# Delta rule of an RWKV-7 branch: the first level of the next pair's inverse moved into the pair ahead, and each chunk's level products issued by themselves

## The reference, cut to what matters

```
def rwkv7_scan(r, w, k, v, kk, a):
    """S_t = S_{t-1}(diag(w_t) - kk_t^T (a_t*kk_t)) + v_t^T k_t ; y_t = S_t r_t. All (B,T,H,N)."""
    def step(S, inp):
        r_t, w_t, k_t, v_t, kk_t, a_t = inp
        sa = jnp.einsum('bhvk,bhk->bhv', S, -kk_t)
        S = (S * w_t[:, :, None, :] + sa[..., None] * (kk_t * a_t)[:, :, None, :]
             + v_t[..., None] * k_t[:, :, None, :])
        y = jnp.einsum('bhvk,bhk->bhv', S, r_t)
        return S, y
```

## Time and profile before

| | |
|---|---|
| Median of 3 executions | 1852.13 us (1851.4 to 1854.01) |
| The profiled execution's own time | 1844.2 us |
| Its span, first to last instruction | 1842.4 us |
| Mean granted TensorE clock | 0.985 |
| Busy: PE, PE weight loads, DVE, ACT, POOL | 1730.4, 1366.7, 1136.0, 822.2, 712.8 us |
| Delta rule of layer 0 | 363.93 to 459.93 us of the span |
| Delta rule of layer 1 | 907.53 to about 1005 us of the span |

### The profile page before, as it was taken

One profiled execution on the slowest core, in us unless ns is written; L12 is line 12 of the kernel. 1 busy time (PEld: TensorE's weight loads), 2 busy tenths in 40 slices (PEclk: granted clock), 3 DMA queues, 4 the chain that ended last, 5 costly groups with the idle time before them and its releaser, 6 DMA issues.

```text
span 1842.4 us, 31964 instructions
## 1 busy us (share of the span) xinstructions
PE 1730.4 (94%) x12808; PEld 1366.7 (74%) x12808; DVE 1136.0 (62%) x1515; ACT 822.2 (45%) x1233; POOL 712.8 (39%) x488
## 2 busy tenths in 40 slices
PE   7999999978998999999978997999998999999996
PEld 7778777767776777777777774666777888887875
DVE  6676787775666127977765745568728364636454
ACT  3443655543635344655533625367634333323342
POOL 2565443320343435633310451433444434334342
PEclk9999999999998999999999998999999999999998
DMA  9772222200532422223201422312243212122222
GB/s 359 268 262 79 92 97 87 93 26 4 196 98 78 152 78 80 92 87 104 76 27 57 163 93 88 151 57 69 80 146 129 92 59 86 65 78 80 69 92 103
DMA packets 63188, 193.01 MB, mean 105 GB/s; under 512 B 5936, under 2 KB 6192, under 8 KB 62672
## 3 DMA queue, kind: packets, MB, share of 16 engines
q1 hardware_dynamic: 63056, 191.10, 30.7%
HBM read 173.25 MB, written 17.83 MB: 104 GB/s over the span
## 4 chain that ended last, share of the span: by engine, by line
PE 60%; issue 21%; POOL 8%; DVE 7%; ACT 4%; POOLq 0%; DVEq 0%; ACTq 0%
PE proj L2417 40%; POOL w_lo_sb L705 7%; PE aux L2436 4%; PE aux L2684 2%; DVE area_sb L1415 2%; PE aux L2597 1%; PE aux L2447 1%; DVE slots_sb L1418 1%; PE aux L3135 1%; PE aux L3141 1%; PE proj L2684 1%; PE aux L2458 1%; PE aux L3132 1%; DVE slots_sb L1415 1%; DVE slots_sb L2107 1%
## 5 line engine op out<-in xcount | busy, mean ns | idle before, releaser
L705 POOL TENSOR_TENSOR w_lo_sb<-w_raw_sb,w_hi_sb 128x512 fp32r<-128x512 f32 x462 | 687.8, 1510 | 986.1 <-ACT w_hi_sb L796 986.1
L2417 PE MATMUL proj<-act_hi_sb,w_hi_sb 128*128 128x512 f32 x1480 | 600.7, 406 | 9.1 <-ACT stage_sb L1209 2.6
L2417 PE MATMUL proj<-act_hi_sb,w_lo_sb 128*128 128x512 f32 x1480 | 578.3, 391 | 0.0
L2417 PE MATMUL proj<-act_lo_sb,w_hi_sb 128*128 128x512 f32 x1480 | 576.9, 390 | 0.0
L796 ACT ACTIVATE w_hi_sb<-w_raw_sb 128x1024 fp32r<-128x1024 f32 x231 | 244.2, 1057 | 658.4 <-PE proj L2417 480.7
L2417 PEld LDWEIGHTS proj<-act_hi_sb,w_hi_sb 128*128 128x128 f32 x1480 | 278.3, 188 | 90.7 <-issue 27.8
L2417 PEld LDWEIGHTS proj<-act_lo_sb,w_hi_sb 128*128 128x128 f32 x1480 | 278.6, 188 | 61.8 <-issue 7.7
L2417 PEld LDWEIGHTS proj<-act_hi_sb,w_lo_sb 128*128 128x128 f32 x1480 | 278.1, 188 | 59.8
L2436 PE MATMUL aux<-act_hi_sb,w_hi_sb 128*128 128x512 f32 x336 | 138.1, 411 | 23.7 <-issue 18.2
L1415 DVE TENSOR_TENSOR area_sb<-area_sb 128x256 f32<-128x256 f32 (+1 forms) x180 | 118.1, 699 | 44.6 <-PE aux L2598 26.7
L2436 PE MATMUL aux<-act_lo_sb,w_hi_sb 128*128 128x512 f32 x336 | 133.9, 399 | 0.0
(11 more groups left out here) (316 smaller groups left out, 2293.0 us busy)
## 6 DMA issues: line engine op xcount, KB each, us to landing
w_raw_sb<-wall SPq DMA_DIRECT2D x231, 512.0 KB, 3.4
area_sb<-w_ada SPq DMA_DIRECT2D x32, 512.0 KB, 5.1
slots_sb<-w_ada SPq DMA_DIRECT2D x32, 256.0 KB, 7.4
gate_scr<-stage_sb SPq DMA_DIRECT2D x32, 256.0 KB, 2.2
area_sb<-gate_scr SPq DMA_DIRECT2D x8, 1024.0 KB, 9.0
x_scr<-area_sb SPq DMA_DIRECT2D x3, 2048.0 KB, 7.8
area_sb<-x_scr SPq DMA_DIRECT2D x2, 2048.0 KB, 13.2
area_sb<-lru_gates SPq DMA_DIRECT2D x1, 3584.0 KB, 11.7
```

Source lines behind the costliest of these rows:

```text
L705: nc.gpsimd.tensor_tensor(w_lo[:, b % 2, :, :].rearrange("p k n -> p (k n)")[:, half], w_raw[:, b % 2, half], w_hi[:, b % 2, :, :].rearran ...
L2417: ins = MM(bank, w[:, s, k, :], a[:, t, :], start=(start and i == 0), stop=(stop and i == len(terms) - 1))
```

## The change

Three things change in the delta rule.

First, level 0 of the next pair (its z and x) is computed within the pair ahead of it, and in the opening for the first pair. For that the masked scores `m1` get a third buffer, `mask_scores` of the next pair moves from the end of a pair into its middle, and the banks 2 and 3 (now `NEXT`) hold the next pair's scores and level-0 z.

Second, the level products of the two chunks are no longer one `beside` call on four corners. Each chunk's product is a call of its own on two corners, with its own waits.

Third, the small steps are placed anew: `key_scores` and `mask_keys` early in the pair, `tokens` in two halves that go through bank 4 one after the other, `u_sb` in two buffers, `state_step(c)` after the level-1 x, both outputs after the level-3 z, and on DVE a wait for the copied xt ahead of the first transposes of a pair.

```
--- before.py
+++ after.py
@@ -228,51 +228,55 @@
...
-        INVERSE, TURNED = (0, 1), (2, 3)
+        INVERSE, NEXT = (0, 1), (2, 3)
...
         for n in range(2, RW_CHUNKS, 2):
             c = n - 2
-            both("z", n, 0, banks=INVERSE)
             jobs.add(("rhs", l, c), 6)
-            both("x", n, 0, banks=INVERSE)
+            both("z", n, 1, banks=INVERSE)
+            both("sk", n, banks=NEXT)
             jobs.add(("u", l, c), 5)
-            both("z", n, 1, banks=INVERSE)
+            both("x", n, 1, banks=INVERSE)
             jobs.add(("st", l, c), 7)
-            both("x", n, 1, banks=INVERSE)
+            jobs.add(("tok", l, n, 0), 4)
+            both("z", n, 2, banks=INVERSE)
             jobs.add(("rhs", l, c + 1), 6)
-            both("z", n, 2, banks=INVERSE)
+            if n + 2 < RW_CHUNKS:
+                both("sb", n + 2, banks=NEXT)
+            both("x", n, 2, banks=INVERSE)
+            jobs.add(("tok", l, n, 1), 4)
+            both("z", n, 3, banks=INVERSE)
+            jobs.add(("u", l, c + 1), 5)
             jobs.add(("y", l, c), 4)
-            both("x", n, 2, banks=INVERSE)
             jobs.add(("y", l, c + 1), 6)
-            jobs.add(("u", l, c + 1), 5)
+            both("x", n, 3, banks=INVERSE)
+            if n + 2 < RW_CHUNKS:
+                both("z", n + 2, 0, banks=NEXT)
             jobs.add(("st", l, c + 1), 7)
-            both("z", n, 3, banks=INVERSE)
-            both("sk", n, banks=(4, 5))
-            both("x", n, 3, banks=INVERSE)
-            for m in range(2):
-                jobs.add(("tok", l, n, m), TURNED[m])
             both("z", n, 4, banks=INVERSE)
             if n + 2 < RW_CHUNKS:
-                both("sb", n + 2, banks=(5, 6))
-            both("xt", n, 4, banks=TURNED)
+                both("x", n + 2, 0, banks=INVERSE)
+            both("xt", n, 4, banks=NEXT)
         for name, bank in (("rhs", 6), ("st", 7), ("y", 4), ("u", 5)):
             jobs.add((name, l, RW_CHUNKS - 2), bank)
...
         R_PART, A_PART = slice(0, 64), slice(64, 128)
-        m1 = [[heads(tiles(2 * k + e), P) for e in range(2)] for k in range(2)]
...
         state_end, rhs_sb = (heads(tiles(22)[:, 256 * e:256 * e + 256], 64) for e in range(2))
-        u_sb = heads(tiles(23)[:, 0:256], 64)
...
                 def pair(i):
                     n, c = 2 * i + 2, 2 * i
                     take(rhs_sb, ("rhs", l, c))
-                    grown(n, 0)
-                    take(u_sb, ("u", l, c))
+                    take(u_sb[0], ("u", l, c))
                     grown(n, 1)
+                    tokens_taken(n, 0)
+                    grown(n, 2)
                     take(rhs_sb, ("rhs", l, c + 1))
+                    tokens_taken(n, 1)
+                    take(u_sb[1], ("u", l, c + 1))
+                    grown(n, 3)
                     take_y(c)
-                    grown(n, 2)
-                    take(u_sb, ("u", l, c + 1))
-                    grown(n, 3)
                     take_y(c + 1)
-                    tokens_taken(n)
+                    if n + 2 < RW_CHUNKS:
+                        grown(n + 2, 0)
                     turned_inverse(n)
 
                 def closing(c):
                     take(rhs_sb, ("rhs", l, c))
-                    take(u_sb, ("u", l, c))
+                    take(u_sb[0], ("u", l, c))
                     take_y(c)
                     take(rhs_sb, ("rhs", l, c + 1))
-                    take(u_sb, ("u", l, c + 1))
+                    take(u_sb[1], ("u", l, c + 1))
                     take_y(c + 1)
...
                     grown, across = tiles(8), tiles(9)
+                    if n and k == 0:
+                        for e in range(2):
+                            job_ready(dve, ("xt", l, n - 2 + e, 4))
                     evacuated_job(dve, ("x", l, n, k))
                     nc.vector.transpose(across[:, 0:256], grown[:, 0:256]).then_inc(S("turned"), 1)
                     evacuated_job(dve, ("x", l, n + 1, k))
@@ -1842,31 +1850,35 @@
                     dve.wait_ge(S("ones_set"), 3 * l + 3)
                     turned(0, 2)
                     levels(0, 3)
+                    mask_scores(2)
                     turned(0, 3)
+                    mask_scores(3)
                     levels(0, 4)
-                    mask_scores(2)
-                    mask_scores(3)
+                    levels(2, 0)
 
                 def pair(i):
                     n, c = 2 * i + 2, 2 * i
-                    levels(n, 0)
+                    more = n + 2 < RW_CHUNKS
                     turned(n, 0)
                     levels(n, 1)
+                    mask_keys(n)
+                    mask_keys(n + 1)
                     next_state(c)
                     turned(n, 1)
                     levels(n, 2)
                     end_state(c)
+                    if more:
+                        mask_scores(n + 2)
                     turned(n, 2)
                     levels(n, 3)
+                    if more:
+                        mask_scores(n + 3)
                     next_state(c + 1)
-                    mask_keys(n)
-                    mask_keys(n + 1)
                     turned(n, 3)
+                    if more:
+                        levels(n + 2, 0)
+                    levels(n, 4)
                     end_state(c + 1)
-                    levels(n, 4)
-                    if n + 2 < RW_CHUNKS:
-                        mask_scores(n + 2)
-                        mask_scores(n + 3)
 
...
                 def inverse_level(n, k):
 
-                    names = [("z", l, n + e, k) for e in range(2)]
-                    parts = []
                     for e in range(2):
                         if k:
                             evacuated_job(pe, ("x", l, n + e, k - 1))
@@ -2740,12 +2749,9 @@
                             evacuated_job(pe, ("sb", l, n + e))
                             pe.wait_ge(S("first_turned"), RW_CHUNKS * l + n + e + 1)
                         x = x_next[e] if k else both(x_one[e])[0]
-                        parts.append((job_open(pe, names[e])[:, 0:256], e == 1 and k > 0,
-                                      of(m1[n // 2 % 2][e], A_PART), of(x), True, True))
-                        if k == 0:
-                            signalled(beside(parts[e]), names[e])
-                    if k:
-                        signalled(beside(*parts), *names)
+                        name = ("z", l, n + e, k)
+                        signalled(beside((job_open(pe, name)[:, 0:256], e == 1 and k > 0,
+                                          of(m1[n // 2 % 3][e], A_PART), of(x), True, True)), name)
 
                 def inverse_turned(n, k, e):
...
@@ -2870,56 +2870,62 @@
                     inverse_level(0, 1)
                     values(2)
                     grow(0, 1)
+                    for m in range(2):
+                        tokens(0, m)
                     inverse_level(0, 2)
-                    tokens(0)
                     grow(0, 2)
+                    upper_scores(2)
+                    values(4)
                     inverse_level(0, 3)
-                    values(4)
+                    values(6)
                     grow(0, 3)
-                    values(6)
                     inverse_level(0, 4)
-                    upper_scores(2)
+                    inverse_level(2, 0)
+                    grow(2, 0)
                     turn_inverse(0)
 
                 def pair(i):
                     n, c = 2 * i + 2, 2 * i
-                    inverse_level(n, 0)
+                    more = n + 2 < RW_CHUNKS
                     right_side(c)
-                    grow(n, 0)
+                    inverse_level(n, 1)
+                    key_scores(n)
                     chunk_updates(c)
-                    inverse_level(n, 1)
+                    grow(n, 1)
                     state_step(c)
-                    grow(n, 1)
+                    tokens(n, 0)
+                    inverse_level(n, 2)
 
                     evacuated_job(pe, ("st", l, c))
                     right = half_bank(("rhs", l, c + 1))
                     state_added(beside((right, True, *state_side(c + 1), True, False))[0], c + 1)
-                    inverse_level(n, 2)
+                    if more:
+                        upper_scores(n + 2)
+                    grow(n, 2)
                     after_state(c + 1)
                     signalled(beside((right, False, *keyed_side(c + 1), False, True)), ("rhs", l, c + 1))
+                    tokens(n, 1)
+                    inverse_level(n, 3)
+                    chunk_updates(c + 1)
                     chunk_output(c)
-                    grow(n, 2)
                     out = half_bank(("y", l, c + 1))
                     old_output(c + 1, out)
-                    chunk_updates(c + 1)
-
+                    grow(n, 3)
+                    if more:
+                        inverse_level(n + 2, 0)
+
+                    evacuated_job(pe, ("u", l, c + 1))
```

(10 more changed lines are left out.)

82 lines of the change are left out of this document (39 added, 43 removed).

## The result

The changed kernel takes 1837.86 us (median of 4 executions, 1837.31 to 1839.59), the kernel before 1852.29 us beside it (4 executions): ratio 0.9918, 95% interval 0.9901 to 0.9935. That is 14.4 us less. 1846.2 was predicted, with a range from 1840.0, so the time lies outside it, on the fast side. The profiled execution took 1838.0 us; its span and the engines' busy time stand on the page (compare).

The account below looks back on a forecast made before the run. PE was taken to bound the whole kernel, a chain across engines the delta rules. Openings -3.2, four pairs -4.0 and last pairs +1.3 gave -5.9 us: 1846.2 us from the median, with an 8-in-10 range of 1840 to 1851.5.

Parts of the forecast that it names:

- the walk: Step-by-step timing of the delta rules: openings -3.2, four pairs -4.0, last pairs +1.3, in sum -5.9 us.
- The periods: Sign for pairs: z1 to z1 takes 20.4 to 21 us; above 21.5 would show the forecast wrong.
- The last pairs: Last pair of each layer: 17.4 us from z1 to the closing's right side, a loss of 1.3 us in the sum.
- Transposes that wait for xt: Sign of being wrong, in a pair: DVE's new wait for xt was to end with its copy at 8.5 us.
- The held groups: PE products held with no releaser named: fewer and shorter after the change, 0.2 us allowed for each pair.
- the clock: Openings: PE may or may not fall to 1.2 GHz, 2 us either way, put in the range only.
- the base: The whole kernel: the gain was set on the runs' median, 7.9 us above the profiled execution's 1844.2 us.
- the split: Level products split by chunk: gains some 0.2 us a half level where PE is free, nothing elsewhere.
- The wait for bank 4: In a pair, y(c) waits for ACT's second token copies to leave bank 4; PE starts it at 10.15 us.
- Larger gain: Rival: overlap at five more places a pair and no holds remaining, 6 us more, 1840 us; chance 0.14.
- Slower: Rival: DVE and ACT work between levels falls on the chain, 1864 us, decided from a 23.2 us period; chance 0.10.
- no change: Rival: two corners give no overlap, each split costs PE 0.45 us, 1851.3 us; chance 0.24.

Follow-up runs that it names:

- the later state update: Changed kernel with DVE's `next_state` moved behind the transposes at both places of a pair: 1832.91 us, repeated 1836.43 us.
- the second trace: A repeat profile without edit: the changed kernel again took 1837.13 us; the kernel before again took 1854.13 us.
- The fillers: Kernel before with eight matmuls that nothing reads added in PE's idle time of each opening: 1849.64 us, ratio 0.9984.
- the early start: Split products, each issued when its own chunk's input is ready, against waiting for both: 1843.19 us in the old order, 1837.86 in the new.
- the split alone: Kernel before with only the level products from level 1 on split by chunk, order and banks as before: 1843.19 us, ratio 0.9945.
- joint waits: Split products issued only after both chunks' inputs are ready: in the kernel before (old order) 1851.89 us, in the changed kernel (new order) 1843.59 us.
- the other bank: Changed kernel with output banks exchanged, y(c) in bank 6 and y(c+1) in bank 4: 1837.20 us, repeated 1839.22 us.

## Why the prediction was wrong

**What was right.** The direction, and much of the walk. In layer 0's second pair z1 to x3 took 11.7 us (12.1 said) and x3 to the next z1 8.6 (8.6 said). x0 waits for z4's copies (1.52 us at 429.85). `next_state` ahead of the transposes holds DVE, as its rows show: it was priced into the walk, and the later state update has it back in its traces.

**The marks it set.** The periods are 20.1 to 20.8 us, three of the four below the 20.4 to 21 named. Level 1 of the first pair came 24.4 us after the stage's start, not 25.5. The last pairs grew by 1.8 us together where 1.3 was said, but with 18.9 and 16.4 us neither is in the range of 17 to 17.6, and in the second trace they take 1.3 less: that sum is luck. Transposes that wait for xt were named as a sign of being wrong and are there (1.57 us at 431.92), though the walk itself had such a wait. The held groups became fewer and shorter, as said.

**The step that failed: "the clock".** "That is 2 us either way, in the range": it was put around zero and not in the sum. In fact the kernel before loses 2.0 us of its first trace and 6.6 of its second to stretches at 1.2 GHz in the delta rules, and by the mean clock of 65 executions the second is the usual one. The changed kernel loses none in its first trace, and its PE is busier there, 18.1 to 18.6 us of 20.1 to 20.8 in a pair where it was 17.4 to 17.9 of some 21.8. So the change takes 5 to 7 us of clock out of the median, by the estimate above, where the sum had nothing. The fillers show that filled idle time keeps the clock up in the openings. That the same holds in the pairs is argued from their busy time and from the traces, and no run fills the pairs alone.

**With it, the base.** The prediction took 5.9 us from a median with a walk made on a trace that lay 7.9 us below it. Of the second trace's 9.9 us over the first, 4.6 lie in the delta rules and are the clock, and these the change takes away; the 5.3 outside stay. The sum made against the first trace's own time gave 1838.3, and 1838.0 was measured, but by two errors that cancel: the walk and the clock gave 4.9 us more than the 5.9 said, and the time outside the delta rules was 4.6 us longer than in the first trace (1654.9 against 1650.3).

**The term that was mis-sized: the split.** "Some 0.2 us a half level where PE is free and nothing where it isn't." Measured: a level of the opening shrinks by 0.5 us, four pairs by 1.9 and 2.5 us, and the early start is worth 6 to 10 us in all, in either order. The step saw that DVE and ACT take the first chunk while the second runs, and priced it too low. By clean stretches the walk gave -8.8 us (190.1 to 181.3) where -5.9 was said: openings -4.8 (said -3.2), pairs -5.6 (-4.0), last pairs +1.8 (+1.3), closings -0.2. In the opening the walk gave the split 0.5 us and the order the rest of its 1.6; the split alone takes 2.0 us off each opening, and the order adds 0.8 in both together. What the walk and the clock missed, 2.9 and 5 to 7 us, makes 8 to 10 us; the forecast was off by 8.3.

**What stays open: the held groups.** The walk counted on 0.2 us of holds in a pair. The idle time without a releaser in the four pairs fell by 6.5 us, more than the 5.6 by which they shortened. The two pieces of the change each lower it: 6.9 us in the pairs with joint waits in the old order, 5.1 with the early start, 3.1 with joint waits in the new order, 2.0 with both. It could be part of how they act, or a shift of the places that any edit makes, as the fillers' pairs suggest. No run tried it.

**The wait for bank 4** was forecast as a new wait of PE until y(c) at 10.15 us. y(c) starts 9.85 us after z1, straight behind u(c+1); ACT's last token copy, from 421.43 for 0.38 us, had just ended. PE shows no idle time before it, and the times with the other bank show no gain.

**The rivals.** "Larger gain" gave 1840, nearly the time. It counted on five more places of overlap, which no run isolates, and on holds that vanish, which they nearly did; the larger worth of the early start and the clock, which the runs do show, were not in it. "Slower" and "no change" have nothing for them; the longest period in both traces was 21.4 us (second trace, layer 1's first pair), far from 23.2. For "no change" the prediction had drawn on the Trainium skill (TensorE: Matmul & The Clock Gate, section The mechanism), by whose strict order each split would cost 0.45 us. That cost does not follow from it: the same section draws matmuls on different tiles overlapping, each starting after the one before.

## What to carry to other kernels

When a product serves two chunks and an in-order engine behind it works them one after the other, issue the first chunk's part as soon as its own input is there: what counts is when the first result comes, and half the rate on PE was worth paying here, though with joint waits in the old order the split gained nothing. Before a forecast is set on a median, compare two traces by stage, with the granted clock of each: in a chain of small products with idle PE time, one trace can lie 8 us from the median, and a change that fills the idle time can take the clock's share with it. The mean granted clock of all executions tells which trace is the usual one. An update that waits for a slow producer should stand behind the work that is ready, not ahead of it.

## What the runs showed of the hardware

- The clock fell in single pairs of a kind in which PE is busy for 17 to 18 of 22 us when it does not fall. Each pair so hit was 1.5 to 1.8 us longer in the kernel before. The places differ between two executions of the same kernel, which makes 4.6 us in the delta rules (192.1 and 196.7).
- Eight useless products in the idle time of each opening gained 3 us (ratio 0.9984).
- Two products on different corners, each a call of its own, overlap in part. The timeline of PE in the changed kernel's second pair: two places with a z of two chunks and what follows it, and a held group:

```profile
412.64 0.32 PE L2696 MATMUL aux<-slots_sb 64*64 64x128 f32 x1
412.69 0.28 PE L2696 MATMUL aux<-area_sb 64*64 64x64 f32 x3
...
416.72 0.97 PE L2696 MATMUL aux<-area_sb 64*64 64x64 f32 x32
417.53 0.46 PE L2696 MATMUL proj<-area_sb,slots_sb 64*64 64x64 f32 x10
...
425.20 0.68 PE L2696 MATMUL aux<-area_sb 64*64 64x64 f32 x16 [0.23 <-issue]
```

The right side behind the z of 416.72 starts after 0.81 us, where one call on four corners takes 0.49 and twice one corner 0.94. With a product of 128 rows behind, it is 0.91 with both inputs ready (379.76 to 380.67 in the joint-waits kernel, above). The Trainium skill (TensorE: Matmul & The Clock Gate, section The mechanism) has matmuls start in strict order. The trace agrees only in part: at 412.64 a first matmul of the key scores starts, and three of the z that the program has ahead of it start at 412.69.
- Groups of products are still held with no releaser shown: the 0.23 us above, up to 1.22 before. In all it was 12.2 us in the delta rules of the kernel before and 4.2 in the changed one. No run tried what holds them.
